# Products with a moving side of 64 columns or less, split by stationary side into two halves of 64

## What is computed

```
# first block, each of 2 layers: three branches of width 512 from one input projection
o_rwkv: for 8 heads of width 64, over 512 steps t:
    sa = S @ a_t
    S  = S * w_t + sa (x) b_t + v_t (x) k_t
    y_t = S @ r_t
o_ret:  chunkwise retention, 4 heads of width 128
o_pool: causal window means and a small linear map
x = x + gate * (sum_n sigmoid(gates_n) * (o_n @ w_branch_n)) @ w_out

# second block, each of 2 layers
x = LN(a*x + 0.5*swiglu(x)); x = LN(a*x + mixer(x)); x = LN(a*x + 0.5*swiglu(x))
# mixer: short conv, wide conv, and attention in a band: 8 query heads of 64,
#        blocks of 128 queries against 2 or 3 blocks of 128 keys
```

## Time and profile before

| what | value |
|---|---|
| median of 3 runs | 3479.86 us (3476.91 to 3484.4) |
| the profiled execution | 3478.07 us, its span 3476.3 us |
| TensorE, matmuls in flight | 3324.5 us, 96% of the span, 16,776 passes |
| VectorE, ScalarE, GpSimd | 1725.2, 1097.7 and 155.7 us |
| mean granted TensorE clock | 0.986 of full speed |
| DMA | 303 MB, 87 GB/s |

### The profile page before, as it was taken

The page is one execution under the profiler, slowest core; times in us unless marked ns, Lnnn a source line. Parts: engine busy times, 40 slices in busy tenths (PEclk is TensorE's granted clock), DMA queues, the critical chain, the costliest instruction groups (busy, mean ns, idle before and its releaser), DMA issues. The chain is left out here.

```text
span 3476.3 us, 42443 instructions
## 1 busy us (share of the span) xinstructions
PE 3324.5 (96%) x16776; PEld 2714.8 (78%) x16776; DVE 1725.2 (50%) x2526; ACT 1097.7 (32%) x1615; POOL 155.7 (4%) x204
## 2 busy tenths in 40 slices
PE   6999899989999999999999999999999999999999
PEld 5778777867777788778888768888888887678887
DVE  6655654456545553463333775332533337753334
ACT  4442223224432322333321343332233213433321
POOL 1000000001000000000000000000000001000000
PEclk9999999999999999999999999999999999999999
DMA  5222122232221111222332211333222322113232
GB/s 225 73 86 97 67 68 79 66 107 99 79 85 61 61 43 55 85 85 97 98 109 85 97 43 62 103 97 109 86 97 97 109 91 97 37 63 102 97 109 79
DMA packets 83494, 303.13 MB, mean 87 GB/s; under 512 B 9680, under 2 KB 9952, under 8 KB 83296
## 3 DMA queue, kind: packets, MB, share of 16 engines
q1 hardware_dynamic: 78064, 283.11, 24.1%
q0 software_dynamic: 5232, 17.31, 1.5%
HBM read 295.66 MB, written 4.72 MB: 86 GB/s over the span
## 5 line engine op out<-in xcount | busy, mean ns | idle before, releaser
L574 PE MATMUL bank<-hh,whi 128*128 128x512 f32 (+1 forms) x2704 | 1070.0, 396 | 26.4 <-DVE tmp L1210 8.4
L576 PE MATMUL bank<-hh,wlo 128*128 128x512 f32 (+1 forms) x2704 | 1029.3, 381 | 0.0
L575 PE MATMUL bank<-hl,whi 128*128 128x512 f32 (+1 forms) x2704 | 1027.1, 380 | 0.0
L1210 DVE TENSOR_TENSOR wlo<-raw,whi 128x1024 fp32r<-128x1024 f32 x498 | 610.4, 1226 | 757.7 <-ACT whi L2141 711.4
L2141 ACT CAST whi<-raw 128x1024 fp32r<-128x1024 f32 x498 | 523.4, 1051 | 731.4 <-PE bank L576 672.4
L574 PEld LDWEIGHTS bank<-hh,whi 128*128 128x128 f32 x2704 | 515.0, 190 | 155.0 <-issue 47.8
L576 PEld LDWEIGHTS bank<-hh,wlo 128*128 128x128 f32 x2704 | 514.1, 190 | 97.3
L575 PEld LDWEIGHTS bank<-hl,whi 128*128 128x128 f32 x2704 | 515.4, 191 | 80.1 <-issue 1.9
L574 PE MATMUL bank<-whi,fh 128*128 128x512 f32 x704 | 274.4, 390 | 0.0
L576 PE MATMUL bank<-whi,fl 128*128 128x512 f32 x704 | 273.9, 389 | 0.0
L575 PE MATMUL bank<-wlo,fh 128*128 128x512 f32 x704 | 273.9, 389 | 0.0
(11 more groups left out here) (321 smaller groups left out, 3708.8 us busy)
## 6 DMA issues: line engine op xcount, KB each, us to landing
raw<-in_W SPq DMA_DIRECT2D x514, 512.0 KB, 3.3
bc<-in_ln_g POOLq DMA_DIRECT2D x6, 512.0 KB, 4.1
bc<-in_ln_b POOLq DMA_DIRECT2D x6, 512.0 KB, 5.6
xn<-in_x SPq DMA_DIRECT2D x4, 512.0 KB, 8.7
mrg<-in_W SPq DMA_DIRECT2D x2, 1024.0 KB, 12.7
AR<-in_W SPq DMA_DIRECT2D x2, 1024.0 KB, 17.8
xn<-in_x POOLq DMA_DIRECT2D x4, 512.0 KB, 5.3
xd<-xn POOLq DMA_DIRECT2D x4, 512.0 KB, 3.6
```

The lines of the kernel that those rows point to most:

```text
L574: e.matmul(out, ah, bh, start=first, stop=False, skip_group_check=True)
L575: e.matmul(out, ah, bl, start=False, stop=False, skip_group_check=True)
L576: return e.matmul(out, al, bh, start=False, stop=last, skip_group_check=True)
L1210: return self.e.tensor_tensor(o, a, b, op)
```

## The change

Each product of `four`, `cW`, `cY`, `per_head` and `values` becomes two: columns q to q + 63 of the stationary side, for q = 0 and 64, with the result in partitions q to q + 63 of the same columns of the bank. Both read the same moving side. The helper `PARTS` lists (i, q) with q inside. `cK`, `from_state`, `grams`, the transposes and the three-product projections stay as they are. The results and all other engines' instructions are the same.

```diff
+PARTS = tuple((i, q) for i in range(4) for q in (0, 64))
...
@@ per_head
-        for c in range(4):
-            t = self.e.matmul(bank[:, 2 * c:2 * c + 2], x[:, c * 128:(c + 1) * 128], sel, start=True, stop=True,
+        for c, q in PARTS:
+            t = self.e.matmul(bank[q:q + 64, 2 * c:2 * c + 2], x[:, c * 128 + q:c * 128 + q + 64], sel, start=True, stop=True,
                               skip_group_check=True)
@@ four
-        for i in range(4):
-            t = self.e.matmul(bank[:, i * 64:(i + 1) * 64], lhs(i), rhs(i), start=True, stop=True, skip_group_check=True)
+        for i, q in PARTS:
+            t = self.e.matmul(bank[q:q + 64, i * 64:(i + 1) * 64], lhs(i)[:, q:q + 64], rhs(i), start=True, stop=True,
+                              skip_group_check=True)
@@ chunk, cW
-        for i, (h, p, q) in enumerate(heads):
-            t = e.matmul(bank[:, i * 64:(i + 1) * 64], G4[:, i * 512 + 256:i * 512 + 384], vn(h), start=c == 0, stop=True,
-                         skip_group_check=True)
+        for i, q in PARTS:
+            t = e.matmul(bank[q:q + 64, i * 64:(i + 1) * 64], G4[:, i * 512 + 256 + q:i * 512 + 320 + q], vn(heads[i][0]),
+                         start=c == 0, stop=True, skip_group_check=True)
@@ chunk, cY
-        for i, (h, p, q) in enumerate(heads):
-            o = bank[:, i * 64:(i + 1) * 64]
-            e.matmul(o, G4[:, i * 512 + 128:i * 512 + 256], SA(i), start=c == 0, stop=False, skip_group_check=True)
-            t = e.matmul(o, G4[:, i * 512 + 384:i * 512 + 512], vn(h), start=False, stop=True, skip_group_check=True)
+        for i, (h, _, _) in enumerate(heads):
+            for n, x in ((128, SA(i)), (384, vn(h))):
+                for q in (0, 64):
+                    t = e.matmul(bank[q:q + 64, i * 64:(i + 1) * 64], G4[:, i * 512 + n + q:i * 512 + n + q + 64], x,
+                                 start=c == 0 and n == 128, stop=n == 384, skip_group_check=True)
@@ values
-            for j in range(nk):
-                t = self.e.matmul(out[:, h * 64:(h + 1) * 64], pT[:, j * 128:(j + 1) * 128],
+            for j, r in itertools.product(range(nk), (0, 64)):
+                t = self.e.matmul(out[r:r + 64, h * 64:(h + 1) * 64], pT[:, j * 128 + r:j * 128 + r + 64],
                                   k.v2[:, (k0 + j) * 128 + kvh * 64:(k0 + j) * 128 + kvh * 64 + 64], start=j == 0,
                                   stop=j == nk - 1, skip_group_check=True)
```

## The result

The changed kernel takes 3442.23 us (median of 4 runs, 3440.74 to 3442.63), the kernel before 3481.0 beside it. The ratio is 0.9891, with a 95% interval of 0.9878 to 0.9903: 38 us less. The forecast was 3466, 14 less, with a range from 3450.

A forecast was written before the change was run, and what follows sets the result against it. TensorE, with matmuls in flight 96% of the span, was taken as the bound. Terms of -10.8, -8.8, -0.5, -0.7 and +8.6 gave -12.2 us, with 2 for earlier results -14: 3479.9 to 3466 us, range 3450 to 3490.

The forecast's parts named there:

- `L899`, 208 groups: Groups of four products in the chunk parts: 148 gain 0.02 us each, 60 late ones 0.13, together 10.8 us less.
- `L974`/`L975`, with `L965`/`L966` and the gap behind `L943`: Sixteen groups of eight products: 0.45 us less each in 12, 0.85 less in the other 4, together 8.8 us less.
- `L951`: Sixteen groups of four products, most behind the carried state's products: 0.89 us becomes 0.20 + 0.66, 0.5 us less.
- `L893`: Sixteen groups of four products: 14 gain 0.02 us, the first of each layer 0.23, together 0.7 us less.
- `L1196`: Attention's values, 64 groups: 0.18 us more each with two products, 0.09 more with three, together 8.6 us more.
- results sooner: Level-step results out some 0.16 us earlier, shortening 21 waits of transposes' loads for `U`: 3.4 us at most, 2 taken.
- clock outside the chunk parts: Not in the sum; as a rival, new gaps bring a third more 1.2 GHz stretches, 16 us, 3482, chance 0.04.
- the size of a split group: Eight pairs behind a 512-column product: 0.32 us ahead, then 0.66 to the next full-width load, 0.98 in a level step.
- the pair rate of 0.058: Two halves side by side take 0.058 us per pair, the lower bound; the upper bound, in turn, was 0.116.
- the slower rival: Halves hinder one another: 3503 at 15 ns more per pair, 3611 fully in turn; chance 0.10 a little, 0.03 in full.
- The gap ahead: Ahead of a split group behind a 512-column product, the first load is not hidden and the array runs empty: 0.32 us.
- "The chain gains more": Rival: earlier results remove a third of 37 us idle, or attention's loss lies beside its waits; 3454 to 3457, chance 0.13.

The follow-up runs named there:

- run alone: Kernel before with only that row's products split: level steps and cS 3455.5 us, cY 3470.4 us, attention's values 3483.9 us.
- the other side: Changed kernel with the attention's values whole again: 3442.5 us, ratio 0.9888 against the kernel before.
- the second profile: The changed kernel as it is, run and profiled once more: 3442.7 us, ratio 0.9892 against the kernel before.
- Experiment 3: Changed kernel with all products of one half ahead of all of the other in each split group: 3504.9 us, ratio 1.0075 against the kernel before.
- experiments 3 and 4: Experiment 3, and then the kernel before with only the last product of each group of four split: 3515.9 us, ratio 1.0104.
- experiment 1: Kernel before with only the products of `four` split (level steps and cS, 208 groups): 3455.5 us, ratio 0.9935.
- experiment 6: Kernel before with `cY` alone split, 16 groups of eight products: 3470.4 us, ratio 0.9968.
- experiment 8: Changed kernel with carried state's products in halves, `cK` with halves in turn, values whole: 3439.1 us, ratio 0.9876 against the kernel before.

## Why the prediction was wrong in size

The steps, as the prediction put them, against sums over the groups of the two traces (each from the start of the product ahead to the next full-width load):

| step | forecast, us | groups, us | run alone |
|---|---|---|---|
| `L899`, 208 groups | -10.8 | -21.8 | -23.8 |
| `L974`/`L975`, with `L965`/`L966` and the gap behind `L943` | -8.8 | -9.4 | -11 |
| `L951` | -0.5 | -1.2 | |
| `L893` | -0.7 | -0.2 | |
| `L1196` | +8.6 | +5.4 | +2, and 0 from the other side |
| results sooner | -2 | not shown; about -5 is left of 37.2 between the level steps, -3 in the second profile | |
| clock outside the chunk parts | 0 | at most -3.5 | |

- **The step that failed is the size of a split group**, "From first load to next full-width load it is 0.66 us for 8 pairs, so 8 x 0.058 = 0.46 and 0.20 fixed". I took `cK` for the very shape that the change makes. The shape is the same, but the order isn't: `cK` issues four passes of one half and then four of the other, the change two and two. Experiment 3 shows that this order is worth up to 0.28 us per group. With 0.615 in the place of 0.66, and with 1.017 for a whole group in the place of the one row with 1.00, a level step is worth 0.077 and not 0.02. Multiplied by 208, a few hundredths are 12 us; the sum of the groups has 11. That is not quite half of the 24 us between 14 and 38, and alone it would have given 3455, inside the range. Out of it the time came by four smaller things together: 3 us of the same mistake at the values, some 3 more than forecast in what is left between the level steps, at most 3.5 of the clock, and 1 to 2 at `cW` and `cY`.
- **Right:** the pair rate of 0.058, with a moving side that both halves share, and with steps; it was the unknown on which the slower rival stood, and the rival is out (16 loads in 0.55 us in the fence of the level step). The gap ahead, 0.32 forecast and 0.33 seen. What is fixed per group made most of the possible gain void: by doubling alone it would have been 139 us less. The Trainium skill, TensorEngine Tiling (Array Packing), Theoretical Speedup, gives up to a factor of two for a side of 64 or less; experiments 3 and 4, both slower than before, show how far from it one can end. The Trainium skill, TensorE: Matmul & The Clock Gate, Part 3, says that loads overlap matmuls only where the row group differs. The level step above speaks against it: all its passes have the same 128 rows, and its 16 loads of 0.14 us start within 0.41 us of one another, while its matmuls are in flight (0.69 us from 287.15 on).
- **`cY`** came as put, 9.4 for 8.8, with 0.505 for 0.45 where a state is carried and 0.848 for 0.85 where `cY` merges with `cK`.
- **The values** cost 5.4 by the groups: 0.707 for 0.569 with two key blocks and 0.824 for 0.793 with three, where 0.75 and 0.87 were forecast. It is the same mistake of 0.05 per group, which made a gain too small at the level steps and makes a loss too large here. The time shows 0 to 2 of the 5.4; the prediction named waits as a cover and didn't think of the clock, which was put as a rival for worse, not for better.
- **The rivals.** "The chain gains more" (3454 to 3457) was nearest in number but not in cause: experiment 1 leaves the chain a few us. The waits that the forecast named, those of the transposes' loads for `U` behind `L1739`, were 21 with 11.4 us and are 20 with 10.5, so they gave 1 of the 2 us put on them. Which waits hold the 3 to 5 us that are left stays open.

The forecast's range was built around the pair rate and reached 24 us up and 16 down. The fixed part, from a single group with another order, had no bounds at all, and should have had them: the nearest row is not the same thing.

## What to carry to other kernels

Splitting a narrow product by its stationary columns pays by the length of the run: here two changes between the full-width array and its halves cost 0.30 to 0.35 us together, each whole pass of 64 moving columns saves 0.053, and a run of eight passes comes out 0.08 ahead, one of six 0.03 behind, one of four 0.14 behind. Let the halves alternate product by product; with one half after the other the same split is slower than none. When a price of some hundredths is multiplied by hundreds of groups, take it as a middle value over many groups with the same order, not from one row.

## What was not expected of the hardware

- Passes of two halves run side by side the more, the nearer they stand to one another in the program: sixteen took 0.615 us from first load to next full-width load when the halves alternate every two passes, 0.66 every four, 0.896 every eight.
- Four quarters of 32 columns run four abreast: 32 passes in 0.584 us, 0.056 for each four with 64 moving columns.
- With only 2 moving columns (`per_head`) the pair rate is 0.058 as well, and it is 0.564 from first load to next full-width load. Before the split the same products took 0.111 per pass, as those with 64 moving columns did, so the stationary columns and not the moving ones set the rate there.
- The time at 1.2 GHz went from 66 us (experiment 3) to 120 us (experiment 6) of the span, and it moves between executions of one kernel too (some 27 us in experiment 8). Where TensorE has work throughout, half of it is lost to 0.1 us: the stretch between the attentions. An edit that saves a few us can be hidden by it or made to look better.
